# Output phase of a hybrid layer: small TensorE work placed between product groups, fp16 halves double-buffered

## What is computed

```
o  = concat([rms_norm(y) * gn_rnn, rms_norm(a) * gn_attn]) @ w_out      # y: recurrence, a: attention, 512 columns each
x1 = layer_norm(alpha * x + gate * o) * ln1_g + ln1_b
h2 = layer_norm_plain(x1) * (1 + scale) + shift
logits = h2 @ [router_g, router_e] + router_b                            # 36 columns
```

## Time and profile before

| | |
|---|---|
| median of three runs | 2208.11 us |
| span of the profiled execution | 2208.1 us |
| PE busy over the span | 84% |
| DVE / ACT / POOL busy | 68% / 47% / 18% |
| output phase in the span | about 848 to 1158 us |

### The profile page before, as it was taken

One profiled execution on the slowest core, in us unless ns is written; L12 is line 12 of the kernel. 1 busy time (PEld: TensorE's weight loads), 2 busy tenths in 40 slices (PEclk: granted clock), 3 DMA queues, 4 the chain that ended last, 5 costly groups with the idle time before them and its releaser, 6 DMA issues. The chain is left out here.

```text
span 2208.1 us, 41507 instructions
## 1 busy us (share of the span) xinstructions
PE 1847.0 (84%) x11836; PEld 1047.0 (47%) x11837; DVE 1498.4 (68%) x1859; ACT 1036.7 (47%) x1360; POOL 388.5 (18%) x375
## 2 busy tenths in 40 slices
PE   2488988889489996999971799999999988989946
PEld 0066666534277774555540345455444444445422
DVE  2357676388789995777669626656758888765537
ACT  1044434577478885222210514544646766543326
POOL 0000000000012211222212112222322323222213
PEclk7689999999799997988975799999999999999979
DMA  9712121276351111333323738778879999986637
GB/s 369 290 58 96 57 85 58 106 246 230 134 196 57 62 52 58 124 114 122 124 77 118 267 67 282 221 225 291 295 230 375 377 370 379 329 285 179 213 83 266
DMA packets 167722, 417.63 MB, mean 189 GB/s; under 512 B 16160, under 2 KB 24768, under 8 KB 163952
## 3 DMA queue, kind: packets, MB, share of 16 engines
q1 hardware_dynamic: 152832, 362.87, 44.9%
q0 software_dynamic: 14832, 54.01, 10.0%
HBM read 343.39 MB, written 73.45 MB: 189 GB/s over the span
## 5 line engine op out<-in xcount | busy, mean ns | idle before, releaser
L1946 PE MATMUL ps<-arena 128*128 x1200 | 459.3, 383 | 43.3 <-DVE arena L1866 43.1
L1866 DVE SCALAR_TENSOR_TENSOR arena<-arena 128x2048 f32 (+1 forms) x186 | 421.1, 2289 | 107.3 <-ACT arena L1810 49.9
L1947 PE MATMUL ps<-arena 128*128 x1200 | 458.9, 382 | 0.0
L1948 PE MATMUL ps<-arena 128*128 x1200 | 458.5, 382 | 0.0
L1804 ACT ACTIVATE arena<-arena 128x2048 f32 (+1 forms) x124 | 233.2, 1908 | 154.1 <-DMA arena<-w 67.9
L618 PE MATMUL ps<-arena 128*128 128x256 f16 (+1 forms) x1680 | 237.7, 303 | 21.1 <-DVE arena L503 21.1
L618 PEld LDWEIGHTS ps<-arena 128*128 128x128 f16 x1680 | 165.8, 100 | 87.3 <-DVE arena L503 15.2
L1946 PEld LDWEIGHTS ps<-arena 128*128 128x128 f16 x1200 | 118.1, 98 | 185.2 <-issue 59.5
L1948 PEld LDWEIGHTS ps<-arena 128*128 128x128 f16 x1200 | 118.4, 99 | 140.7 <-issue 4.5
L1947 PEld LDWEIGHTS ps<-arena 128*128 128x128 f16 x1200 | 118.1, 98 | 131.8 <-issue 4.0
L1810 ACT ACTIVATE arena<-arena 128x2048 f32 (+1 forms) x62 | 117.4, 1908 | 68.7 <-DMA arena<-w 50.6
(11 more groups left out here) (287 smaller groups left out, 3040.5 us busy)
## 6 DMA issues: line engine op xcount, KB each, us to landing
arena<-w SPq DMA_DIRECT2D x186, 1024.0 KB, 12.9
arena<-hT_d SPq DMA_DIRECT2D x64, 512.0 KB, 6.0
arena<-w_mod SPq DMA_DIRECT2D x12, 2048.0 KB, 17.2
h_d<-arena SPq DMA_DIRECT2D x17, 512.0 KB, 3.0
x_d<-arena SPq DMA_DIRECT2D x17, 512.0 KB, 2.6
arena<-x SPq DMA_DIRECT2D x8, 1024.0 KB, 6.3
hT_d<-arena SPq DMA_DIRECT2D x16, 512.0 KB, 3.7
arena<-x SPq DMA_DIRECT2D x16, 512.0 KB, 4.7
```

The source lines that it names most:

```text
L1866: return nc.vector.scalar_tensor_tensor(dst, src, scale, high, ALU.mult, ALU.subtract)
L1946: pe.matmul(out, high, part(buf, whi, at, 512), start=first, stop=False)
L1947: pe.matmul(out, high, part(buf, wlo, at, 512), start=False, stop=False)
L1948: return pe.matmul(out, low, part(buf, whi, at, 512), start=False, stop=last)
```

## The change

The order inside `phase_output` is rewritten; the arithmetic is the same.

- PE: the product of tile t is cut into its 8 row blocks. Behind block 0 stand the sums and the transposes of tile t+1, behind 1 and 2 the two halves of the transposes of `h2` of tile t-2, behind 3 and 4 the two halves of its router step. The sum over partitions goes to column 64 of bank 7 in place of bank 0.
- The fp16 halves have two buffers, by parity of the tile, so they can be made while the product of the tile before runs.
- A new semaphore `o_y` is raised when the recurrent half of the product (blocks 0 to 3) is done; ACT's copy to `t0` waits for it in place of `o_mm`. DVE's L1312 now waits for `o_mm` itself.
- DVE makes the low halves of tile t+1 and adds the router's bias of tile t-2 at the two places of `normalise(t-1)` where it waits for POOL.
- ACT's order per step is `prepare(t+1)`, `route(t-2)`, `scaled(t)`.
- At the start of the phase only four row blocks of the weights are split before tile 0 is prepared; PE waits for each block by itself.
- SP loads `y` and `a` of both first tiles ahead of `x`, and refills `y` and `a` a tile earlier than it stores.

The diff, cut to the order; its pieces are, in this order, common code, SP, POOL, DVE, ACT and PE.

```diff
-    def tiles(eng, prepare, project, normalise, route):
+    def tiles(eng, first, step, finish):
...
-    yhi, ylo, ahi, alo = (b[n].bitcast(F16) for n in ("yhi", "ylo", "ahi", "alo"))
+    yhi, ylo, ahi, alo = ([b[f"{n}{j}"].bitcast(F16) for j in range(2)] for n in ("yhi", "ylo", "ahi", "alo"))
...
+            refill(0, 0)
+            for t in range(T_LAT):
+                if t + 3 < T_LAT:
+                    refill(t + 1, 1 - t % 2)
+                stores(t, t % 2)
+                if t + 2 < T_LAT:
+                    load_x(t + 2, t % 2)
...
+            def step(t, j):
+                if known(t, 1):
+                    normalise(t - 1, 1 - j)
+                if has_next(t):
+                    prepare(t + 1, 1 - j)
...
-            def prepare(t, j):
-                dve.wait_ge(hi, START + 2 * t + 1)
-                dve.wait_ge(o_mm, START + t)
-                nc.vector.scalar_tensor_tensor(ylo, b[f"yT{j}"], X_SCALE, yhi, ALU.mult, ALU.subtract).then_inc(lo, 1)
+            def low_y(t, j):
+                dve.wait_ge(hi, START + 2 * t + 1)
+                if known(t, 2):
+                    dve.wait_ge(o_y, START + t - 1)
+                nc.vector.scalar_tensor_tensor(ylo[j], b[f"yT{j}"], X_SCALE, yhi[j], ALU.mult, ALU.subtract).then_inc(lo, 1)
...
+            def first():
+                nc.vector.tensor_scalar(b["sc2"], b["sc2"], 1.0, None, ALU.add).then_inc(w_ok, 1)
+                for k in range(C_RNN):
+                    split_w(k)
+                low_y(0, 0)
+                low_a(0, 0)
+                squares(0, 0)
+                for k in range(C_RNN, KD):
+                    split_w(k)
+                dve.wait_ge(w_ok, START + 1)
+            def step(t, j):
+                def first_wait():
+                    if has_next(t):
+                        low_y(t + 1, 1 - j)
+                def second_wait():
+                    if has_next(t):
+                        low_a(t + 1, 1 - j)
+                    if known(t, 2):
+                        route(t - 2)
+                if known(t, 1):
+                    normalise(t - 1, 1 - j, first_wait, second_wait)
...
+                if has_next(t):
+                    squares(t + 1, 1 - j)
...
+            def first():
+                for k in range(C_RNN):
+                    high_w(k)
+                prepare(0, 0)
+                for k in range(C_RNN, KD):
+                    high_w(k)
+            def step(t, j):
+                if has_next(t):
+                    prepare(t + 1, 1 - j)
+                if known(t, 2):
+                    route(t - 2)
+                scaled(t, j)
...
+            def step(t, j):
+                product(t, j, 0)
+                if has_next(t):
+                    column_sums(t + 1)
+                    transposes_a(t + 1, 1 - j)
+                product(t, j, 1)
+                if known(t, 2):
+                    transposes_h(t - 2, j, 0)
+                product(t, j, 2)
+                if known(t, 2):
+                    transposes_h(t - 2, j, 1)
+                product(t, j, 3)
+                if known(t, 2):
+                    router(t - 2, 0)
+                product(t, j, 4)
+                if known(t, 2):
+                    router(t - 2, 1)
+                product(t, j, 5)
+                product(t, j, 6)
+                product(t, j, 7)
```

More of the change, by code:

```diff
@@ L1191, in phase_output @@
     NV = 14
-    def tiles(eng, prepare, project, normalise, route):
[L1195 to L1205, removed]
+    def tiles(eng, first, step, finish):
+        first()
+        step(0, 0)
+        step(1, 1)
         with eng.Fori(1, T_LAT // 2 - 1) as i:
@@ L1209, in tiles, with known, has_next @@
         step(T_LAT - 2, 0)
[L1210 to L1216, removed]
+        step(T_LAT - 1, 1)
+        finish()
+    def known(t, low):
+        return not isinstance(t, int) or t >= low
+    def has_next(t):
+        return not isinstance(t, int) or t + 1 < T_LAT
     def half(t):
@@ L1275, in normalise, with split_w @@
                     nc.gpsimd.tensor_tensor(rs, ve, b["mh"][:, 0:1], ALU.pow).then_inc(pw, 1)
-            tiles(pool, prepare, none, normalise, none)
+            def step(t, j):
[3 more added lines that the diff above has]
+                    prepare(t + 1, 1 - j)
+            tiles(pool, lambda: prepare(0, 0), step, lambda: normalise(T_LAT - 1, 1))
         @block.vector
         def _(dve):
-            nc.vector.tensor_scalar(b["sc2"], b["sc2"], 1.0, None, ALU.add).then_inc(w_ok, 1)
-            dve.wait_ge(w_ok, START + 1)
-            for k in range(KD):
+            def split_w(k):
                 dve.wait_ge(w_hi, START + k + 1)
@@ L1409, in project @@
                         pe.wait_ge(o_act, START + t)
[L1410 removed]
+                    elif known(t, 1):
                         pe.wait_ge(v, START + NV * t - NV + 1)
[L1412 to L1418 removed]
@@ L1436, in _ @@
-            tiles(pe, prepare, project, none, route)
+                if not known(t, 1):
+                    pe.wait_ge(w_lo, START + k + 1)
+                for n in range(2):
+                    o, cols = ps[:, bank + n, :], slice(n * 512, (n + 1) * 512)
+                    lhs_hi, lhs_lo = high[:, at * P:(at + 1) * P], low[:, at * P:(at + 1) * P]
+                    pe.matmul(o, lhs_hi, whi[:, k, cols], start=(at == 0), stop=False)
+                    pe.matmul(o, lhs_hi, wlo[:, k, cols], start=False, stop=False)
+                    mm = pe.matmul(o, lhs_lo, whi[:, k, cols], start=False, stop=(at == C_RNN - 1))
@@ L1439, with finish @@
+            def finish():
+                for t in (T_LAT - 2, T_LAT - 1):
+                    for n in range(2):
+                        transposes_h(t, t % 2, n)
+                    for n in range(2):
+                        router(t, n)
+            tiles(pe, first, step, finish)
 W13 = 2 * KD * D_EXP
```

141 lines of the change are left out of this document (81 added, 60 removed).

## The result

The changed kernel takes 2150.57 us (median of 4 runs, 2147.54 to 2153.08) against 2206.53 (4 runs, 2204.58 to 2208.21): 0.9742 of the time before, 95% interval 0.9727 to 0.9758. 2157 was forecast, within 2149 to 2182. The profiled execution took 2147.54, of which its span is 2145.7.

The account below looks back on a forecast made before the run. PE was taken to bound the output phase. Savings of 44.1 us between first and last product, 2.8 at the start and 4.6 at the end, together 51.5, took 2208.1 to 2156.6, say 2157 us; range 2149 to 2182.

Parts of the forecast that it names:

- The turn on PE: Steady output-phase turn: product, transposes, sums and router at full-clock cost with PE never waiting, 14.47 us.
- the middle: From tile 1's first product to tile 15's product end: 212.9 us against 256.97, 44.1 us less.
- The clock: Steady turns: no clock loss, as the longest part without product shrinks from 5.76 to 1.36 us.
- The row I leaned on: Tile 1's turn before the change: clock stayed at 1.00 through 2.90 us without product, PE idle for half.
- The exchange: Four more places per turn where PE goes from fp16 products to fp32 work and back: price taken as 0.
- rivals 3 and 4: Cut order holds PE: 3, gain mostly eaten, 2198 us, chance 0.06; 4, slower than before, 2217 us, chance 0.04.
- Rival 1: PE's clock keeps falling once per turn in the output phase: 23 us more, 2180 us; chance 0.12.
- DVE: DVE's step, normalise plus inserted pieces partly filling its waits for POOL: 13.3 us, so PE stays the bound.
- Rival 2: DVE becomes the bound, its inserted pieces adding to its waits: 14.8 us per turn, 2162 us; chance 0.08.
- The start: Start of the output phase: tile 1's product starts 2.8 us earlier, between 1.5 and 5.
- The gap of 2.5 us: PE idles behind block 0 of tile 0, as ACT reaches tile 1's squares only after four weight blocks.
- The end: After tile 15's product: 18.2 us in place of 22.8, 4.6 us less, with tile 13's router inside the product.

Follow-up runs that it names:

- e1: Changed kernel with PE's small work in one row behind the whole product, no cutting, buffers and signals kept; 2159.11 us.
- e11: Kernel before, with 7 useless fp16 matmuls per turn ahead of PE's waits for the h2 transposes and the router; 2179.23 us.
- e5: e1 with two waits of the kernel before put back, ahead of the h2 transposes and the router; 2214.78 us.
- e10: Kernel before, with the sums moved to bank 7 and the router's first half starting behind ACT's first copy of h2T; 2170.49 us.
- e2: Changed kernel, but ACT's copy of the recurrent half to t0 waits for the end of the whole product; 2171.28 us.
- e3: Changed kernel, but the fp16 halves of y have one buffer while those of a keep two; 2202.56 us.
- e12: Kernel before, with only the sums moved to bank 7, removing the wait ahead of the h2 transposes; 2193.98 us.
- e13: Kernel before, with only the router's wait changed: its first half starts behind ACT's first copy of h2T; 2182.31 us.
- e6: Changed kernel with PE's small work cut into eight groups instead of five, one behind every block; 2146.27 us.
- e4: Changed kernel, but DVE makes the low halves and the router's bias behind normalise, not in its waits for POOL; 2154.3 us.
- e7: Changed kernel, but at the start ACT makes tile 1's squares and high half of y ahead of the last four weight blocks; 2148.14 us.

## Why the prediction was right, and where its reason was not

**The turn on PE: right.** 14.47 forecast, 14.14 found. The order of the sum holds; three terms were 0.08 to 0.18 us too large: sums 0.82 for 0.93, `h2` 0.86 for 0.94, router 1.62 for 1.80. Over 13 turns that is 4.3 of the 4.6 us by which the middle came out better (208.3 for 212.9).

**The clock: right value, failed step.** "The fall comes once per turn, each time after the long part without product" is what failed, and with it "after the change the longest part without product is sums plus transposes, 1.36 us" as the reason to take no loss. `e1` has 4.56 us without product and 1.00; `e11` 5.29 us with fillers and 1.00; `e5` puts two waits back and has 0.87. What brings the clock down here are PE's idle gaps among the fp32 groups between two products: 0.34 + 0.81 us in the earlier trace rows, taken away in `e10` (0.99) and put back in `e5`. The change removed these too (sums in bank 7, router in halves, ACT's copies made while a block runs), so the time came out as forecast for a partly wrong reason. Had the change cut the product without closing the gaps, I would have added their idle time and no loss of clock; that case was not run. The gaps closed and no cutting is `e1`: 2186 by my reason, 2159 on the chip.

The row I leaned on, did not separate the two: tile 1's turn held the clock with PE idle for half of 2.90 us, but it had no router step in it. `e2` (1.29 us idle once a turn, between the last matmul of one product and the first of the next, clock 1.00) and `e3` (2.44 us, clock down in five turns) show that the length of a gap alone doesn't decide either. `e12` and `e13`, with one gap each still in place, land at 0.90 and 0.95. In `e13` and `e3` turns of one shape run with the clock up and with it down. Which mixture of idle time and small fp32 work is enough stays open.

The Trainium skill's rule (page "TensorE: Matmul & The Clock Gate", section "A second HAM failure mode: psum-queue depth-cycling"), by which short idle gaps between groups of matmuls make the clock go down and up, agrees with the trace of before, with `e5` and with `e11`. It has no size for the gaps, and not every short gap does this: `e1` (0.44 us) and `e2` (1.29 us) stay at 1.00. I had read it as speaking against the change. It doesn't, since in after the groups have no gaps between them: 160.00 us of PE busy in 160.00.

**The exchange: right.** It was put at nothing, and the turn of 14.14 leaves no room for a price; `e6` with eight groups in place of five has a shorter turn still. So rivals 3 and 4 fall. Rival 1 falls with the clock at 1.00.

**DVE: right by less than forecast.** The step was put at 13.3 and is 13.95. Left out were about 0.2 us each before L1293, L1299, L1304 and L1321 (an instruction that needs the one before it) and the 0.4 us of every second step; some 0.3 come back, as L1293 and L1299 take 0.61 from start to next start and not the 0.69 shown. The gap before L1321 was missed because 12.55 was read at the end of the phase, where L1314 starts 1.31 us behind L1312; in a steady turn of before it is 1.46. The margin to PE is 0.2 us, not 1.2. Rival 2 is what `e4` shows: with the pieces behind `normalise`, DVE's 14.30 bound the turn, for about the price that the rival named.

**The start: mis-sized.** 5.8 us gained for 2.8. After its own beginning, block 0 starts 6.7 us in (forecast 7.6), since the load of `a` landed earlier; sums and transposes took 862.04 - 860.50 = 1.54 for 2.4; the ramp cost 872.63 - 862.04 - 9.07 = 1.5 for 2.5. The last term is in part luck: in `e4`, with the same start, tile 1's product came 25.0 us after the phase and not 23.8. The gap of 2.5 us was foreseen and is 2.19, and `e7` shows it can be avoided.

**The end: right.** 4.5 for 4.6.

**What each part is worth.** Taken from the changed kernel one at a time: the double buffer of y 52 us (`e3`), the signal of the recurrent half 20.7 (`e2`), the cutting 8.5 (`e1`), the places on DVE 3.7 (`e4`). The last is within the scatter of the medians. They don't add up, because the clock falls or stays for all together.

## What to carry to other kernels

Ahead of a plan to reorder PE's work, list PE's idle gaps with what released each, however short, and look at the granted clock behind them; on this kernel 0.90 us of gaps a turn cost 34 us. First take such waits away where they stand (another bank for the result, a wait split in two), or fill them with matmuls into a free bank, and reorder for what is left. When a reason for the clock is read from one stretch, look for a second stretch that differs in only one thing before it is believed.

## What the runs showed of the hardware, unexpected

- Seven useless fp16 matmuls of 384 columns a turn made the kernel before 27.5 us faster (`e11`), as the clock went from 0.88 to 1.00.
- The length of the idle time alone doesn't decide over the clock: 1.29 us once a turn between two fp16 matmuls left it at 1.00 in `e2`, and 0.34 + 0.25 us beside fp32 groups had it down in several turns of `e13` (0.95).
- Small fp32 groups between fp16 products cost less than in a row: a router half 0.81 us and a quarter 0.36 (`e6`), against 1.80 for the whole step in a row.
- A single wait of 2.44 us in every turn (`e3`) let the clock fall in some turns and not in others of the same shape, at 3.4 to 4.8 us each.
- With the same order at the start of the phase, the clock came up at different times in different executions: tile 1's product began 23.8 us after the phase in after and 25.0 in `e4`.
